# Gate rows and a bias spread over the partitions by DMA instead of by float32 products, in a two-block transformer kernel

## What is computed

```python
mod = silu(c) @ ada_w[l] + ada_b[l]          # c is one vector: mod is one row of 6144
shift, scale, gate = split(mod, 3)           # gate: one row of 2048
h = rms_norm(x, norm_g[l]) * (1 + scale) + shift
z = h @ w_in[l]                              # latents, attention gate, conv input, conv gate
attn = causal_attention(...) * silu(mla_gate)        # 256 x 1024
u = causal_depthwise_conv(glu(conv_in), dw_w[l], dw_b[l])
u = silu(layer_norm(u, conv_ln_g[l], conv_ln_b[l]))
u = u @ w_pw[l] + b_pw[l]                    # pointwise product and bias: 256 x 1024
conv_out = u * silu(conv_gate)
y = concatenate([attn, conv_out]) @ w_out[l] # 256 x 2048
x = x + gate * y
```

## Time and profile before

| | us |
|---|---|
| median of 3 runs | 1991.26 |
| lowest and highest of them | 1987.6, 1992.05 |
| the profiled execution, its own time | 1991.99 |
| span in its trace, first to last instruction | 1990.2 |
| TensorE busy in that span | 1953.2 |
| VectorE busy | 1498.4 |
| ScalarE busy | 1019.5 |
| mean granted TensorE clock | 0.992 of full |

### The profile page before, as it was taken

The page is one execution under the profiler, slowest core; times in us unless marked ns, Lnnn a source line. Parts: engine busy times, 40 slices in busy tenths (PEclk is TensorE's granted clock), DMA queues, the critical chain, the costliest instruction groups (busy, mean ns, idle before and its releaser), DMA issues.

```text
span 1990.2 us, 24805 instructions
## 1 busy us (share of the span) xinstructions
PE 1953.2 (98%) x9268; PEld 1630.4 (82%) x9268; DVE 1498.4 (75%) x2014; ACT 1019.5 (51%) x1471; POOL 126.0 (6%) x86
## 2 busy tenths in 40 slices
PE   9999999999999999999999989999999899999998
PEld 7888888888888888888888878888877688888877
DVE  5786787777777676777775568988885778888865
ACT  5545455445444444453444454666654545667452
POOL 1231232000000000000000000101000000011000
PEclk9999999999999999999999999999999999999999
DMA  7787876889888888888896545654544466555444
GB/s 246 238 270 239 274 236 230 274 284 306 269 294 300 284 298 286 294 285 304 276 307 207 192 138 153 193 173 147 162 137 158 134 189 183 168 157 154 159 147 139
DMA packets 225311, 441.95 MB, mean 222 GB/s; under 512 B 15701, under 2 KB 57063, under 8 KB 225191
## 3 DMA queue, kind: packets, MB, share of 16 engines
q1 hardware_dynamic: 224867, 439.93, 68.0%
q10 hardware_dynamic: 324, 0.43, 0.1%
HBM read 438.20 MB, written 2.10 MB: 221 GB/s over the span
## 4 chain that ended last, share of the span: by engine, by line
PE 82%; DVE 6%; issue 6%; ACT 4%; POOL 3%; DMA 0%; POOLq 0%; DVEq 0%; ACTq 0%
PE P L688 25%; PE P L690 25%; PE P L689 25%; PE P L449 2%; DVE WL L1004 2%; POOL ST L1364 2%; DVE CA L1001 1%; PE P L481 1%; POOL QK L1386 1%; ACT WH L987 1%; PE P L558 1%; PE P L568 0%; PE P L569 0%; ACT FB L705 0%; DVE FB L1262 0%
## 5 line engine op out<-in xcount | busy, mean ns | idle before, releaser
L1004 DVE TENSOR_TENSOR WL<-RAW,WH 128x1024 fp32r<-128x1024 f32 x648 | 790.3, 1224 | 336.7 <-ACT WH L987 335.1
L987 ACT ACTIVATE WH<-RAW 128x1024 fp32r<-128x1024 f32 x648 | 671.0, 1045 | 588.2 <-PE P L690 467.1
L688 PE MATMUL P<-WH,AH 128*128 128x512 f32 (+1 forms) x1536 | 604.3, 393 | 3.5 <-DVE WL L1004 3.4
L690 PE MATMUL P<-WH,AL 128*128 128x512 f32 (+1 forms) x1536 | 594.9, 387 | 0.0
L689 PE MATMUL P<-WL,AH 128*128 128x512 f32 (+1 forms) x1536 | 594.0, 387 | 0.0
L688 PE MATMUL P<-WH,BH 128*128 128x512 f32 x896 | 355.1, 396 | 0.0
L690 PE MATMUL P<-WH,BL 128*128 128x512 f32 x896 | 350.8, 392 | 0.0
L689 PE MATMUL P<-WL,BH 128*128 128x512 f32 x896 | 350.3, 391 | 0.0
L688 PEld LDWEIGHTS P<-WH,AH 128*128 128x128 f32 x1536 | 289.5, 188 | 59.8 <-issue 3.9
L690 PEld LDWEIGHTS P<-WH,AL 128*128 128x128 f32 x1536 | 289.0, 188 | 59.0
L689 PEld LDWEIGHTS P<-WL,AH 128*128 128x128 f32 x1536 | 289.6, 189 | 55.4
(11 more groups left out here) (245 smaller groups left out, 1417.4 us busy)
## 6 DMA issues: line engine op xcount, KB each, us to landing
RAW<-in_ada_w_dram SPq DMA_DIRECT2D x192, 512.0 KB, 5.0
RAW<-in_mlp_w_in_dram SPq DMA_DIRECT2D x128, 512.0 KB, 4.6
RAW<-in_mlp_w_out_dram SPq DMA_DIRECT2D x128, 512.0 KB, 5.2
RAW<-in_sb_w_qkv_dram SPq DMA_DIRECT2D x96, 512.0 KB, 4.9
RAW<-in_w_in_dram SPq DMA_DIRECT2D x80, 512.0 KB, 3.8
RAW<-in_w_in_dram SPq DMA_DIRECT2D x128, 256.0 KB, 3.2
RAW<-in_w_out_dram SPq DMA_DIRECT2D x64, 512.0 KB, 3.8
RAW<-in_sb_w_o_dram SPq DMA_DIRECT2D x32, 512.0 KB, 5.4
```

The source lines that it names most:

```text
L688: e.matmul(o, xh, wh, start=st and k == 0, stop=False)
L690: m = e.matmul(o, xl, wh, start=False, stop=u.last and k == u.nk - 1)
L987: e.activation(WH[:, n % NH, 0:size], RAW[:, i % NR, 0:size], ACT.Copy).then_inc(w_high, 1)
L1004: return e.tensor_tensor(o, x, h.bitcast(F32), ALU.subtract)
```

## The change

The gate row now goes through DRAM. When the last of the 12 sums of `mod` for layer l is there, in the middle of the first block, one unit later TensorE turns the 16 gate columns into 16 rows of 128 (one transpose, `gate_row`), ScalarE copies them into a spare corner of `FB` and issues a transfer of 8 KB to a DRAM tensor `gates`. At the end of `z` SP issues a transfer that reads this row once for each partition, 128 x 2048 float32, into `G`, and one that reads `b_pw` 128 times into `BR`, now 128 x 1024. They stand behind SP's load for unit zend+8. `o_add` waits for the first, `p_evict` for the second. The products of lines 627 and 677 and the copies of line 966 are gone; the first matmul of a `p` chunk opens its bank itself. `p_evict` adds the bias to both banks into `MP`, then multiplies by `SCG` from there: four instructions in place of two, and `p_turn` waits for the last of them. The scale of the second block's norm also waits for the transfers to `gates`, so that `FB` is free.

```diff
-            after[s].append(("pw_bias", l))
-            for j in range(4):
-                after[s + j].append(("gate_rows", l, j))
...
+                    if items[-1][1][1] == 5:
+                        after[nxt].append(("gate_row", items[-1][1][0]))
...
-            def gate_rows(l, j):
-                pb = bank(("gate", l, j))
-                if j == 0:
-                    for pc in (4, 5):
-                        e.wait_ge(*T.emptied(("ada", l, pc)))
-                for i in range(4):
-                    gc = MOD[:, l, 32 + 4 * j + i:33 + 4 * j + i].to_broadcast([128, 128])
-                    m = e.matmul(pb[:, i * 128:(i + 1) * 128], gc, IDN, start=True, stop=True)
-                m.then_inc(*T.filled(("gate", l, j)))
+            def gate_row(l):
+                pb = bank(("gate", l))
+                for pc in (4, 5):
+                    e.wait_ge(*T.emptied(("ada", l, pc)))
+                e.transpose(pb[0:16, 0:128], MOD[:, l, 32:48], IDN).then_inc(*T.filled(("gate", l)))
...
-                if st and u.g[0] == "p":
-                    e.wait_ge(s_bias, 16 * (u.g[1] + 1))
-                    for t in range(2):
-                        e.matmul(P[:, 2 * u.pair + t, 0:u.w], ONE[0:1, :], BR[0:1, u.c * 512:(u.c + 1) * 512], start=True, stop=False)
-                    st = False
...
-            def gate_rows(l, j):
-                e.wait_ge(*T.ready(("gate", l, j)))
-                e.activation(G[:, j * 512:(j + 1) * 512], T.ap(("gate", l, j)), ACT.Copy).then_inc(*T.drained(("gate", l, j)))
+            def gate_row(l):
+                row = FB[0:16, 2, l * 128:(l + 1) * 128]
+                e.wait_ge(*T.ready(("gate", l)))
+                e.activation(row, T.ap(("gate", l))[0:16, 0:128], ACT.Copy).then_inc(*T.drained(("gate", l)))
+                e.wait_ge(*T.emptied(("gate", l)))
+                e.dma_start(gates[l, :].rearrange("(r p) -> r p", p=128), row).then_inc(s_row[l], 16)
...
-                for t in range(2):
-                    m = e.tensor_tensor(MP[:, t, :], psum(("p", l), c, t), SCG[:, t, c * 512:(c + 1) * 512], ALU.mult)
-                m.then_inc(pair_emptied[opened[("p", l), c][0]], 1)
+                e.wait_ge(s_bias, 16 * (l + 1))
+                e.tensor_tensor(MP[:, 0, :], psum(("p", l), c, 0), BR[:, c * 512:(c + 1) * 512], ALU.add).then_inc(*p_bias.up(l, c))
+                e.tensor_tensor(MP[:, 1, :], psum(("p", l), c, 1), BR[:, c * 512:(c + 1) * 512], ALU.add).then_inc(pair_emptied[opened[("p", l), c][0]], 1)
+                e.wait_ge(*p_bias.at(l, c))
+                e.tensor_tensor(MP[:, 0, :], MP[:, 0, :], SCG[:, 0, c * 512:(c + 1) * 512], ALU.mult)
+                e.wait_ge(*emptied(("p", l), c))
+                e.tensor_tensor(MP[:, 1, :], MP[:, 1, :], SCG[:, 1, c * 512:(c + 1) * 512], ALU.mult).then_inc(*p_gated.up(l, c))
...
-                e.wait_ge(*T.emptied(("gate", l, c)))
+                e.wait_ge(s_gate, 16 * (l + 1))
...
+            def rows(l):
+                e.wait_ge(s_row[l], 16)
+                e.wait_ge(unit_done, zend[l])
+                e.dma_start(G[:, :], gates[l:l + 1, :].to_broadcast([128, D])).then_inc(s_gate, 16)
+                e.dma_start(BR[:, :], A["b_pw_2"][l:l + 1, :].to_broadcast([128, 1024])).then_inc(s_bias, 16)
...
+                for l in range(2):
+                    if items[i] == ("w", zend[l] + 8):
+                        rows(l)
```

More of the change, by code:

```diff
@@ L167, in build @@
         MP = put("MP", [128, 2, 512], off=oA + 24 * K)
-        BR = put("BR", [1, 1024], off=oA + 28 * K)
+        BR = put("BR", [128, 1024], off=oA + 28 * K)
         U1 = put("U1", [128, 2, 512], off=oBH + 4 * K)
@@ L177, in build @@
         P = ctx.enter_context(nc.psum_tensor("P", [128, 8, 512], F32))
+        gates = nc.dram_tensor("gates", (2, D), F32).ap()
         vload, late, col = [], [], {"norm_mix_g": VC[:, 0:16]}
@@ L396, in build @@
         s_cst, s_gain, s_vec, s_bias, s_out = sem("consts_in"), sem("gain_in"), sem("vectors_in"), sem("bias_in"), sem("stored")
+        s_row, s_gate = [sem("gate_row0"), sem("gate_row1")], sem("gate_in")
         s_x = [sem(f"x_in{c}") for c in range(4)]
@@ L411, in build @@
         mx, ex, rcp, o_high = tally("score_max"), tally("score_exp"), tally("score_recip"), tally("o_high")
-        conv_d, x_mid = tally("conv"), tally("x_half_added")
+        conv_d, x_mid, p_bias, p_gated = tally("conv"), tally("x_half_added"), tally("p_biased"), tally("p_gated")
         ln_d, ln_a, ln_p, ul_high, ul_low, gact = tally("ln_dve"), tally("ln_square"), tally("ln_rstd"), tally("ul_high"), tally("ul_low"), tally("gate_silu")
@@ L416, in build @@
                    lnexp, tn_mask, a_exp, a_mask, bh_high, hid_sq, hid_high, hid_low, pads, tabs, sig, lat_sq, lat_ms, lat_r, lat_high,
-                   kr_sq, kr_ms, kr_rot, q_sq, q_ms, q_rstd, q_rot, rot, k_sq, k_ms, k_rs, k_nrm, k_rope, rope_zero, mx, ex, rcp, o_high, conv_d, x_mid,
+                   kr_sq, kr_ms, kr_rot, q_sq, q_ms, q_rstd, q_rot, rot, k_sq, k_ms, k_rs, k_nrm, k_rope, rope_zero, mx, ex, rcp, o_high, conv_d, x_mid, p_bias, p_gated,
                    ln_d, ln_a, ln_p, ul_high, ul_low, gact, p_high, x_done]
@@ L618, in ln_scale @@
                 m.then_inc(*T.filled(("lnr", l)))
-            def gate_rows(l, j):
-                pb = bank(("gate", l, j))
-                if j == 0:
-                    for pc in (4, 5):
-                        e.wait_ge(*T.emptied(("ada", l, pc)))
-                for i in range(4):
-                    gc = MOD[:, l, 32 + 4 * j + i:33 + 4 * j + i].to_broadcast([128, 128])
-                    m = e.matmul(pb[:, i * 128:(i + 1) * 128], gc, IDN, start=True, stop=True)
-                m.then_inc(*T.filled(("gate", l, j)))
+            def gate_row(l):
[3 more added lines that the diff above has]
+                e.transpose(pb[0:16, 0:128], MOD[:, l, 32:48], IDN).then_inc(*T.filled(("gate", l)))
             def p_turn(l, c, i):
                 pb = bank(("pt2", l, c, i))
-                e.wait_ge(*emptied(("p", l), c))
+                e.wait_ge(*p_gated.at(l, c))
                 turn(pb, MP, 0, 2 * i)
@@ L638, in tensor_program @@
                          att_flip=att_flip, att_out=att_out, att_back=att_back, ln_mean=ln_mean, ln_var=ln_var, ln_scale=ln_scale,
-                         gate_rows=gate_rows, p_turn=p_turn)
+                         gate_row=gate_row, p_turn=p_turn)
             def await_rows(g, k):
@@ L942, in ln_centre @@
                     e.activation(SQL[:, cp, :], flat(CA[:, 2 * cp:2 * cp + 2, :]), ACT.Square).then_inc(*ln_a.up(l, cp))
-            def pw_bias(l):
-                e.wait_ge(unit_done, zend[l])
-                e.dma_start(BR[0:1, :], A["b_pw_2"][l:l + 1, :]).then_inc(s_bias, 16)
             def ln_act(l, cp):
@@ L975, in scalar_program @@
                          z_evict=z_evict, glu=glu, lat_turn=lat_turn, q_evict=q_evict, k_evict=k_evict, k_scale=k_scale, att_turn=att_turn, att_scores=att_scores,
-                         att_flip=att_flip, att_back=att_back, ln_centre=ln_centre, pw_bias=pw_bias, ln_act=ln_act, gate_act=gate_act,
-                         gate_rows=gate_rows, p_turn=p_turn)
+                         att_flip=att_flip, att_back=att_back, ln_centre=ln_centre, ln_act=ln_act, gate_act=gate_act,
+                         gate_row=gate_row, p_turn=p_turn)
             def highs(step):
@@ L1106, in mod_scale @@
                 e.wait_ge(unit_done, L0[l])
+                e.wait_ge(s_row[l], 16)
+                if l == 0:
+                    e.wait_ge(s_row[1], 16)
                 fma(SCL[:, :], MOD[:, l, 16:32], 1.0, of("norm_g_2", 16, l), ALU.add, ALU.mult).then_inc(*scl.up(l))
```

## The result

| | before | after |
|---|---|---|
| median of the runs, us | 1991.65 (6 runs, 1987.6 to 1992.66) | 1973.92 (6 runs, 1970.66 to 1976.03) |
| the profiled execution's own time, us | 1991.99 | 1973.09 |
| its span, us | 1990.2 | 1971.3 |

The ratio is 0.9914, with a 95% interval from 0.9901 to 0.9927. The forecast was 1975.5, so 16 us of gain; 17.7 were measured in the medians and 18.9 between the two profiled executions.

A forecast was written before the change was run, and what follows sets the result against it. The prediction took TensorE to bound the kernel. From 1991.99 us, -6.0 -8.4 -3.2 +0.4 +1.2 = -16.0 gave 1976.0; with the median of runs 0.7 lower it predicted 1975.5, range 1970.5 to 1983.5.

The forecast's parts named there:

- What bounds the kernel: Whole kernel: TensorE, busy 98% of the span, sets the time; savings count one for one except where it waits.
- Gates, -6.0: Before the layer norm: removing eight gate product groups saves 6.7 us, less 2 x 0.35 lost to VectorE, leaving 6.0.
- Bias products, -8.4: At the openings of `p` chunks: removing bias products at four places behind the layer norm saves 8.4 us.
- The clock behind them, -3.2: Behind layer 0's two bias products: falls to 1.2 GHz vanish, 1.6 us each, 3.2 us; possible 0 to 6.4.
- Transposes, +0.4: First block, TensorE: two added transposes of gate columns cost 0.4 us for both, restarts included.
- Wait at `p_turn`, +1.2: Before each `p` chunk's transposes: longer `p_evict` makes TensorE wait 0.2 and lose 0.1 preloading, 4 x 0.3 us.
- Transfers, hidden: At the end of `z`: `G` lands near 1448.5, wanted about 1450.7, so hidden by 2 us; `BR` wanted much later.
- (b): Transfer into `G`: the spreading read is slow and holds VectorE, 1982.7 at half the gap, 1989.9 whole; chance 0.10.
- (c): Transfer into `G`: the read runs at 60 GB/s, `G` lands 11.5 us late, slower than before at 1998.5; chance 0.04.
- rival (d): Pauses at the layer norm: clock falls move, two more give 1978.7, two fewer 1972.3; chance 0.10.
- The sum: All terms total -16.0 us from 1991.99, so 1976.0; median forecast 1975.5, chance 0.66.
- (a): Ahead of the layer norm: VectorE keeps the pace, the gates' 6.0 us go into TensorE's wait, 1981.5; chance 0.10.

The follow-up runs named there:

- Experiment 1: Changed kernel with the bias back on TensorE as one-partition products and two instructions in `p_evict`, gate change kept: 1983.2 us, ratio 0.9964 to before.
- experiment 2: Changed kernel with the gate products and their copies back and the transfer into `G` out, bias change kept: 1979.55 us, ratio 0.9945 to before.
- Experiment 3: Changed kernel with the bias on TensorE as float32 identity times spread bias over 128 partitions, two instructions in `p_evict`: 1978.2 us, ratio 0.9942 to before.
- experiment 4: Kernel before with each pair of one-partition bias products issued a second time: 2003.68 us, ratio 1.0063 to before.
- experiment 5: Changed kernel with one extra megabyte per layer of the same read ahead of `G` in SyncE's queue: 1978.49 us, ratio 0.9935 to before.
- experiment 6: Changed kernel with three extra megabytes per layer of the same read ahead of `G` in SyncE's queue: 1992.39 us, ratio 1.0013 to before.
- Experiment 7: Changed kernel with the bias addition left out and `p_evict` back to two instructions: 1972.36 us, ratio 0.9907 to before.
- experiment 8: Changed kernel with the layer norm's later steps one unit on and the conv gate's Silu eight units on: 1968.06 us, ratio 0.9885 to before.

## Why the prediction was right, point by point

**What bounds the kernel.** Right. TensorE's busy time and the span went down together (18.6 and 18.9 us).

**Gates, -6.0.** The sign and the mechanism were right, the size was 1.2 short, for two reasons. The restart behind small products was counted at two groups and not at the six that stand behind others; the rows put 0.89 on such a group too, and 8 x 0.89 = 7.1. And the 2 x 0.35 that was to be lost to VectorE was not lost: the first `o_add` is 3.6 us sooner in each layer (3.73 less the 0.13 by which the executions already differ at 1435, and 13.35 - 9.71), and the way from there to the layer norm is as long as before. Walking through VectorE's instructions gave 3.0; the slack of 4.1 us ahead of it took in all 3.6. Experiment 1 shows the same in time, 7.5.

**Bias products, -8.4.** Right. The first place of each layer gives 2.0 up to the next large matmul (2.53 to 4.53, 14.93 to 16.93).

**The clock behind them, -3.2.** Right in sum. From 4.53 to 9.87 in layer 0 is 5.34, of which the same stretch in layer 1 has 2.13 (16.93 to 19.06) without a fall. The rest, 3.2, is the two falls. That they belong to the float32 bias products and do not just drift with time is what experiments 1 to 4 say: behind such products stand seven falls at twelve places (two of four in before, two of four in experiment 1, three of four in experiment 4), and at the 28 places where they are gone or are over 128 partitions there is none (after and experiments 2, 3, 5 to 8, four each). Each kernel stands there with one trace. The Trainium skill's rule (TensorE: Matmul & The Clock Gate, "What's actually happening") puts the fall down to an array that has lately not been busy. At these products the trace counts TensorE as busy throughout: in the earlier trace rows they begin at 1494.30 and last 1.98, and the next matmul starts at 1496.21. Whether it is the single partition that does it is open. Experiment 3 speaks for it, with none of four over 128 partitions. Against it as the only condition speaks a fall in after's first block, behind the eight float32 products of one column, over 128 partitions, that sum the columns of `mod` (TensorE, then a stretch with columns as in the earlier trace rows):

```profile
335.79 1.95 PE L482 MATMUL P<-CST,ADA 128*128 128x1 f32 x16
340.00:342.00 2.00, 2.00 (x7) 1.62 (x6) 1.24 (x1) 0.00 (x0) 0.15 (x1) 0.50 0.61 163
```

TensorE was busy there too, with no pause over 0.1 us before. The same place has a fall in four of the ten traces, and the other eleven such sums have none in any.

**Transposes, +0.4.** Too high. TensorE at the first of them:

```profile
586.32 0.27 PE L625 MATMUL P<-CST,MOD 128*16 128x128 f32 x1
```

From the large matmul ahead to the second one behind it is 0.57 us (586.09 to 586.66), where two steps take 0.46: 0.11. The other, at 1064.71, is alike (1064.48 to 1065.06). So both cost 0.2 us. At 1435 after is even 0.13 ahead of before, with the clock's falls at other places in the first block.

**Wait at `p_turn`, +1.2.** The wait came as described and half as long: 0.11, with 0.03 to 0.04 for the next step, four times 0.15. The four instructions of `p_evict` take 2.48 (1502.76 to 1505.24) and not 2.61. The signal was no quicker than the 0.11 that was put on it: the transposes start 0.15 behind the last instruction, at 1505.39. The bound below, 0, was nearer than the one above. Experiment 7 agrees with 0.11.

**Transfers, hidden.** Right, nearly to the tenth in layer 0: `G` at 1448.6 for a forecast of 1448.5. The cover is 1.4 there and 2.0 in layer 1, for a forecast of 2. Rivals (b) and (c) fall for the transfer as it is, and experiments 5 and 6 show that their price was right. The Trainium skill's 103 GB/s (DMA: Bandwidth & Descriptors, "Latency and other measured facts") did not apply to 128 partitions that read one row. A megabyte at that rate takes 10.2 us, an estimate from the page's figure; here it landed 6.5 and 7.1 us after its issue, and in the stretch in which `G` lands the engines move 371 GB/s in all. The lateness that the prediction worked out from that figure, 4.7 us, was too high by its own times as well: 10.2 us from 1444.9 end at 1455.1, 4.4 behind 1450.7.

**Other falls of the clock.** They came as in rival (d), and cancelled, which was luck. From `o_add` to `ln_scale` layer 0 gives 1.2 back (3.73 to 2.53), where after has two falls and before one; layer 1 gains 1.6 (13.35 to 14.93), where it has one instead of two. Net 0.4 gained. Over the whole trace, start and end aside, the clock is low for 30.7 us in before and for 23.9 in after. The difference, 6.8 us at half clock, is that of the two falls behind the bias products.

**The sum.** Against 16.0: 1.2 more from the gates, 0.8 more from bias and `p_turn` (four places net 8.0 for 7.2), 0.4 not lost up to 1435 and 0.13 gained there, 0.4 from the clock. That is the 18.9 of the two profiled executions. The terms that were off all erred to the same side, and the forecast of 1975.5 was still within 1.6 us of the median. Some of its smaller sums do not come out: 1991.99 - 16.0 - 0.7 is 1975.3, and the bounds of the range are not what the words beside them give. No wait and two falls fewer end at 1971.1 and not at 1970.5; all of (a) and half of (b) together end at 1988.7, and each alone at 1981.5 and 1982.7, so none of them is 1983.5. The measured 1973.92 lies inside on either reading.

## What to carry to other kernels

Where one engine sets the time, price a small operation on it by the distance between the starts of its large neighbours, with the restart counted at every place, and look at the granted clock behind it too: here a pair of products that spread a row cost 2.1 us and the clock behind it as much as 1.6 more. A row can be spread by a transfer as long as its queue is issued early enough; read the cover from the first use, since what is late beyond it is paid one for one. And a gain ahead of a wait for another engine isn't lost when that engine's run begins with the first engine's own work and it has slack before.

## What was not expected of the hardware

- A float32 product over one partition is dearer than one over 128. Net of two ordinary steps of 0.23, a pair costs 2.11 us over one partition (2.57 - 0.46) and 1.71 over 128 (2.17 - 0.46). A second pair over one partition adds only 1.72 (experiment 4), so the extra 0.4 is paid once per place.
- The granted clock falls to 1.2 GHz behind one-partition products, in 7 places of 12, with TensorE counted busy 3.00 of 3.00 us, and behind pauses of 1.2 to 2 us at the layer norm. It also falls, at one place in 4 of 10 traces, behind eight float32 products of one column over 128 partitions, with TensorE counted busy. Which of the places is followed by a fall changes from kernel to kernel.
- A read of one 8 KB row by all partitions, a megabyte, lands in 6.5 to 7.1 us behind a 512 KB load. One more megabyte in the queue ahead of it delays its landing by 3.9 us and three by 10.0, counted from the issue of the 512 KB load ahead of them all (mean of two layers: 7.26, 11.16 and 17.24 us).
